# The even layer's out-projection in halves of its rows, the first half beside the neighbourhood attention

## What is computed

```
def _even_mixer(x, norm_g, w_in, ..., rpb_b, w_out):
    h = _rmsnorm(x, norm_g)
    qa, ka, va, qb, kb, vb = _split(h @ w_in, EVEN_SPLITS)
    ...
    oa = _window_gqa(qa, ka, va, sink_a)            # 8 heads of 64: 512 features
    ...
    ob = _neighbourhood_attn(qb, kb, vb, rpb_b)     # 8 heads of 64: 512 features
    return jnp.concatenate([oa, ob], axis=-1) @ w_out   # 1024 x 1024

x = x + _even_mixer(x, ...)
x = x + _mlp(x, mlp_norm[0], w_mlp_in[0], w_mlp_out[0])
```

## Time and profile before

| what | value |
|---|---|
| median of 3 executions | 2370.2 us (2369.26 to 2370.75) |
| the profiled execution, its own time | 2369.17 us |
| its span in the profile | 2367.3 us |
| TensorE busy | 2210.6 us, 93% |
| VectorE busy | 1052.3 us, 44% |
| ScalarE busy | 847.4 us, 36% |
| GpSimd busy | 813.5 us, 34% |
| mean granted TensorE clock | 0.974 |

### The profile page before, as it was taken

The page is one execution under the profiler, slowest core; times in us unless marked ns, Lnnn a source line. Parts: engine busy times, 40 slices in busy tenths (PEclk is TensorE's granted clock), DMA queues, the critical chain, the costliest instruction groups (busy, mean ns, idle before and its releaser), DMA issues.

```text
span 2367.3 us, 27011 instructions
## 1 busy us (share of the span) xinstructions
PE 2210.6 (93%) x9984; PEld 1730.5 (73%) x9984; DVE 1052.3 (44%) x1542; ACT 847.4 (36%) x1256; POOL 813.5 (34%) x343
## 2 busy tenths in 40 slices
PE   6788989779999998898899999999989998999999
PEld 5676357557888885575678888878878876788887
DVE  3456474557552525347533223235562565322221
ACT  5332343443222223345543323343432443433231
POOL 3222013323444442220244444443324322444443
PEclk9899999999999999999999999999999998999999
DMA  4212013112333233110123233232222211223322
GB/s 141 67 54 72 27 45 98 63 45 80 120 111 95 93 129 101 45 63 19 44 91 98 97 95 94 97 105 76 71 67 89 72 63 63 89 98 98 98 98 98
DMA packets 54966, 193.35 MB, mean 82 GB/s; under 512 B 6096, under 2 KB 6352, under 8 KB 54480
## 3 DMA queue, kind: packets, MB, share of 16 engines
q1 hardware_dynamic: 50400, 181.58, 23.5%
q10 hardware_dynamic: 4464, 10.36, 1.3%
HBM read 189.82 MB, written 2.10 MB: 81 GB/s over the span
## 4 chain that ended last, share of the span: by engine, by line
PE 72%; issue 14%; DVE 9%; POOL 4%; ACT 1%; DMA 0%; POOLq 0%; SPq 0%; DVEq 0%; ACTq 0%
PE gemm_ps L493 21%; PE gemm_ps L495 21%; PE gemm_ps L494 21%; POOL wl L462 4%; PE out_ps L860 2%; DVE tmp L1568 1%; DVE arena L1922 1%; DVE tmp L1929 1%; DVE arena L1568 1%; PE turn_ps L688 1%; PE score_ps L679 1%; DVE x L1590 1%; PE out_ps L698 1%; DVE xl L1568 1%; PE score_ps L852 1%
## 5 line engine op out<-in xcount | busy, mean ns | idle before, releaser
L462 POOL TENSOR_TENSOR wl<-raw,wh 128x1024 fp32r<-128x1024 f32 x339 | 813.3, 2401 | 1535.9 <-ACT wh L1086 1535.8
L493 PE MATMUL gemm_ps<-xh,wh 128*128 128x512 f32 x1512 | 615.6, 407 | 55.5 <-DVE xl L1568 22.7
L1086 ACT ACTIVATE wh<-raw 128x1024 fp32r<-128x1024 f32 x339 | 358.7, 1059 | 772.7 <-DMA raw<-w_in 745.3
L494 PE MATMUL gemm_ps<-xl,wh 128*128 128x512 f32 x1512 | 594.5, 393 | 0.0
L495 PE MATMUL gemm_ps<-xh,wl 128*128 128x512 f32 x1512 | 594.3, 393 | 0.0
L494 PE MATMUL gemm_ps<-arena_r,wh 128*128 128x512 f32 (+1 forms) x1124 | 432.1, 384 | 0.0
L493 PEld LDWEIGHTS gemm_ps<-xh,wh 128*128 128x128 f32 x1512 | 288.0, 190 | 137.6 <-issue 56.3
L493 PE MATMUL gemm_ps<-arena_r,wh 128*128 128x512 f32 (+1 forms) x868 | 334.3, 385 | 11.1 <-DVE arena_r L1573 10.2
L494 PEld LDWEIGHTS gemm_ps<-xl,wh 128*128 128x128 f32 x1512 | 287.6, 190 | 66.9 <-issue 9.0
L495 PE MATMUL gemm_ps<-arena_r,wl 128*128 128x512 f32 (+1 forms) x868 | 332.3, 383 | 0.0
L495 PEld LDWEIGHTS gemm_ps<-xh,wl 128*128 128x128 f32 x1512 | 287.2, 190 | 61.5
(11 more groups left out here) (309 smaller groups left out, 2040.2 us busy)
## 6 DMA issues: line engine op xcount, KB each, us to landing
raw<-w_in SPq DMA_DIRECT2D x339, 512.0 KB, 3.3
arena<-na_in ACTq DMA_DIRECT2D x14, 256.0 KB, 2.7
x<-x_in SPq DMA_DIRECT2D x8, 256.0 KB, 6.4
out<-x ACTq DMA_DIRECT2D x8, 256.0 KB, 2.8
arena<-alibi_in ACTq DMA_DIRECT2D x6, 256.0 KB, 3.3
con<-con_in SPq DMA_DIRECT2D x1, 1432.0 KB, 11.7
arena<-moba_in ACTq DMA_DIRECT2D x1, 1024.0 KB, 4.9
arena<-mem_in ACTq DMA_DIRECT2D x1, 1024.0 KB, 4.9
```

The costliest lines, as they stand in the source:

```text
L462: pool.tensor_tensor(wl[:, k, :], raw[:, k, :], wh[:, k, :].bitcast(F32), ALU.subtract).then_inc(unit_split, 1)
L493: pe.matmul(o, wh[:, n % RING, w], h[:, kt, 0:width], start=(kt == 0), stop=False)
L494: pe.matmul(o, wh[:, n % RING, w], l[:, kt, 0:width], start=False, stop=False)
L1086: act.activation(wh[:, k % RING, :], raw[:, k % RING, :], ACT.Copy).then_inc(high_split, 1)
```

## The change

The weights of the even out-projection are put on the stream in another shape: the first four units hold rows 0 to 511 of `w_out`, the last four rows 512 to 1023, and each unit holds two output blocks (2 x 4 input blocks of 128). The first four units run in sixteen pieces of six matmuls in steps 3 to 18 of the neighbourhood attention: two steps for an output block, block `2u` into bank 0 of `gemm_ps`, block `2u + 1` into bank 1. VectorE adds each finished block to `x` in steps 5, 7, ..., 19, behind its own attention work of the step. The last four units follow the attention, two banks each, and their sums are added to `x` a second time. ScalarE raises the units at steps 2, 8, 12, 16 and 19. The meeting of the engines is left out on all three. TensorE waits for the last add of the first half before the second half, and for the last group's split before the last input block of its first unit. The count of matmuls is the same, 192; `x` is added to 16 times in place of 8.

```diff
--- before.py
+++ after.py
@@ -361,6 +361,8 @@
         unit_split = sem("unit_split")
         unit_done = sem("unit_done")
         emptied = sem("emptied")
+        part_done = sem("part_done")
+        part_emptied = sem("part_emptied")
         block_ready = sem("block_ready")
         high_made = sem("high_made")
         proj_raw = sem("proj_raw")
@@ -1007,17 +1009,53 @@
             take(copied_v, 2)
             out = FIRST["even_out"]
 
+            def half_rows(o, n, part, first, start, end):
+
+                for kt in range(start, end):
+                    w = slice((4 * part + kt) * P, (4 * part + kt + 1) * P)
+                    pe.matmul(o, wh[:, n % RING, w], xh[:, first + kt, :], start=(kt == 0), stop=False)
+                    pe.matmul(o, wh[:, n % RING, w], xl[:, first + kt, :], start=False, stop=False)
+                    m = pe.matmul(o, wl[:, n % RING, w], xh[:, first + kt, :], start=False, stop=(kt == 3))
+                return m
+
             def window_part(i):
 
-                if i in (4, 7, 10, 13):
-                    k = (i - 4) // 3
-                    begun(out + k // 2, 2 * (k % 2), 2 * (k % 2) + 2, xh, xl)
+
+                if 3 <= i < 19:
+                    k, later = divmod(i - 3, 2)
+                    u, part = divmod(k, 2)
+                    n = out + u
+                    if later:
+                        half_rows(gemm_ps[:, part, :], n, part, 0, 2, 4).then_inc(unit_done if part else part_done, 1)
+                        return
+                    if not part:
+                        pe.wait_ge(unit_split, n + 1)
+                        if u:
+                            pe.wait_ge(part_emptied, u)
+                        else:
+                            pe.wait_ge(emptied, out)
+                            pe.wait_ge(rhs_ready, blocks_split[0] + 4)
+                    elif u:
+                        pe.wait_ge(emptied, n)
+                    half_rows(gemm_ps[:, part, :], n, part, 0, 0, 2)
             pair_attention(pair_items("neighbour"), window_part)
             blocks_split[0] += 4
-            meet()
-            for n in (out, out + 1):
-                products(n, KT, xh, xl, N, start=4)
-            units(out + 2, KT - 2, xh, xl)
+            groups = taken[group_used]
+            for n in range(out + 4, out + 8):
+                pe.wait_ge(unit_split, n + 1)
+                pe.wait_ge(emptied, out + 4 if n == out + 4 else n - 1)
+                banks = (score_ps[:, n % 2, :], gemm_ps[:, n % 2, :])
+                if n == out + 4:
+                    pe.wait_ge(group_used, groups - 1)
+                    for part, o in enumerate(banks):
+                        half_rows(o, n, part, 4, 0, 3)
+                    pe.wait_ge(group_used, groups)
+                    for part, o in enumerate(banks):
+                        m = half_rows(o, n, part, 4, 3, 4)
+                else:
+                    for part, o in enumerate(banks):
+                        m = half_rows(o, n, part, 4, 0, 4)
+                m.then_inc(unit_done, 1)
             added_sum()
             units(FIRST["mup0"], 1, mh, ml, fresh=True)
             units(FIRST["mup0"] + 1, 7, mh, ml)
@@ -1505,9 +1543,19 @@
                 if 17 <= i <= 18:
                     copy_values([values_b[:, :, k * P:(k + 1) * P] for k in (2 * (i - 17), 2 * (i - 17) + 1)], gemm_ps)
             pair_attention(pair_items("window"), whole=True, between=prepare_neighbour)
-            pair_attention(pair_items("neighbour"))
-            meet()
-            prepare(x, "mlp0", mh, stored(FIRST["even_out"]), added=True)
+            out_first = FIRST["even_out"]
+
+            def raise_out(i):
+                if i == 2:
+                    raise_to(out_first + 3)
+                if i in (8, 12, 16, 19):
+                    raise_to(out_first + 2 + (i + 1) // 4)
+            pair_attention(pair_items("neighbour"), between=raise_out)
+
+            def second_half(b):
+                raise_to(out_first + 4 + b // 2 + 3)
+                act.wait_ge(emptied, out_first + 4 + b // 2 + 1)
+            prepare(x, "mlp0", mh, second_half, added=True)
             mlp("m", 0)
             for p in (1, 2, 3):
                 mlp("m", p)
@@ -2099,9 +2147,25 @@
             def split_window(i):
                 if i < 4:
                     split(y[:, 5 + i, :], xh[:, i, :], xl[:, i, :], rhs_ready)
+                if 5 <= i < 20 and i % 2:
+                    u, part = divmod((i - 5) // 2, 2)
+                    if part:
+                        dve.wait_ge(unit_done, FIRST["even_out"] + u + 1)
+                    else:
+                        take(part_done)
+                    b = 2 * u + part
+                    done(dve.tensor_tensor(x[:, b, :], x[:, b, :], gemm_ps[:, part, :], ALU.add),
+                         emptied if part else part_emptied)
             pair_attention(pair_items("neighbour"), split_window)
-            meet()
-            add(FIRST["even_out"], "mlp0", mh, ml)
+            for u in range(4):
+                n = FIRST["even_out"] + 4 + u
+                dve.wait_ge(unit_done, n + 1)
+                for b, ps in ((2 * u, score_ps), (2 * u + 1, gemm_ps)):
+                    done(dve.tensor_tensor(x[:, b, :], x[:, b, :], ps[:, n % 2, :], ALU.add),
+                         emptied if b % 2 else dve_step)
+                for b in (2 * u, 2 * u + 1):
+                    low(x, "mlp0", mh, ml, b)
+                    add_square(b)
             inverse()
             mlp("m", 0)
             for p in (1, 2, 3):
@@ -2180,7 +2244,10 @@
     e = inp["w_in_e_2"][0]
     units.append(_blocks(np.concatenate([e[:, :512].reshape(D, 8, HD)[:, pair].reshape(D, 512), e[:, 512:]], 1)))
     e = inp["w_out_e_2"][0]
-    units.append(_blocks(np.concatenate([e[:512].reshape(8, HD, D)[pair].reshape(512, D), e[512:]], 0)))
+    a = _blocks(np.concatenate([e[:512].reshape(8, HD, D)[pair].reshape(512, D), e[512:]], 0))
+
+    a = a.reshape(U_EVEN_OUT // 2, 2, P, 2, 4 * P).transpose(3, 0, 2, 1, 4)
+    units.append(a.reshape(U_EVEN_OUT, P, KT * P))
     parts(FF2_PARTS, [inp["w_mlp_in_2"][0]], inp["w_mlp_out_2"][0])
     o = inp["w_in_o_2"][0]
     q, k, v, g = np.split(o, [D, 2 * D, 4 * D], axis=1)
```

## The result

The changed kernel takes 2376.49 us (median of 9 executions, 2374.07 to 2380.71), the kernel before 2369.26 us (median of 9, 2368.05 to 2374.06). The ratio is 1.0030 with a 95% interval of 1.0022 to 1.0038: slower by 0.3%. Forecast were 2369.0 us and no change that can be measured, with 2375 as the upper end. The profiled execution of the changed kernel took 2374.07 us.

The account below looks back on a forecast made before the run. TensorE was taken to bound the out-projection behind the attention, with 8.2 us of holes beside the attention. -16.3 + 12.0 (attention stretch with seam) + 3.6 (tail) = -0.7 us gave 2369.0 us, range 2364 to 2375.

Parts of the forecast that it names:

- the item for the clock at step 3: Attention start: first new piece starts near 1111.8 us, partly at 1.2 GHz, later ones at 2.4 GHz; +0.5 us.
- the item for GpSimd: Attention stretch: GpSimd's low-part subtractions delay VectorE at steps 8, 12 and 16; bounds 0 and 3.8 us, taken 1.3.
- the last: Rival for the whole change: pieces wait for adds or weights; +5 us or more, 2375 and up, chance 0.05.
- the second: Rival: clock falls in the tail before the mlp; with step-16 collision and full backlog 2373.5 to 2377 us, chance 0.2.
- signs of being wrong: Second half starting before 1167.3 or after 1176 us, or the granted clock falling behind the last unit.
- The 72 matmuls: Out-projection behind the attention: 72 matmuls leave the full stretch at 0.227 us each, -16.3 us, called certain.
- A piece costs 1.58 and the floor: Attention stretch: twelve more pieces at 1.58 us add 19.0; with 10.6 us of holes filled, growth is at least 8.4.
- The output steps: Attention steps where VectorE stands 1.61 us for ScalarE: mostly covered by TensorE's longer steps, 0.4 us left in all.
- The adds, the raises' loads, SP: Attention stretch: eight adds on VectorE (5.5 us), and loads for ScalarE's raises on SP, fit in and cost nothing.
- The seam: Between attention and second half: wait for the first half's last add leaves 1.4 us, where 2.4 stood.
- The tail: Last out-projection unit to the mlp: two-block unit delays the column sums by 2.6 us, plus 1.0 backlog; +3.6 us.
- The backlog on VectorE: Tail: VectorE's 4.3 us of work per 5.4 us unit, plus collisions, delays the last adds; bounds 0 and 2.5, taken 1.0.

Follow-up runs that it names:

- e3: Changed kernel with the first piece's waits split and the step-16 raise moved to step 17: ratio to the kernel before 1.0002, stretch 70.9 us.
- e1: Changed kernel, first half of the first piece waits only for the two blocks it reads: ratio to the kernel before 1.0016, stretch 74.3 us.
- e2: Changed kernel with ScalarE's raise of step 16 moved to step 17, so GpSimd's subtraction follows the last division: ratio to the kernel before 1.0016.
- e4: Changed kernel with the first mlp unit's products over six input blocks ahead of the two column sums: ratio to the kernel before 1.0010, tail 23.9 us.

## Why the prediction was wrong

Two terms of the sum for the attention stretch failed: the item for the clock at step 3, which left out the wait for VectorE's fourth split, and the item for GpSimd. The sum for that stretch was +12.0 us and the trace shows +20.2. The measured time lies where two rivals had put it: the last (2375 and up, chance 0.05), with pieces that wait, though for a split and for divisions and not for adds or weights; and the second (2373.5 to 2377, chance 0.2), with the collision at step 16 and the clock's fall in the tail, though smaller and without the backlog. Two of the signs of being wrong came: the second half starts at 1177.19, behind 1176, and the granted clock falls behind the last unit.

- **The 72 matmuls: right.** The stretch behind the attention went from 38.2 to 21.9 us, -16.3.
- **A piece costs 1.58 and the floor: right.** The piece from 1137.90 to 1139.49 takes 1.59. The 0.2 us above six paces lie at its two ends (0.34 us to its second matmul, 0.33 from its last to the scores); that the switch of operand kinds makes them was argued and is not shown. With the two faults mended (e3) the stretch grew by 11.9 us where the sum said 12.0. The waits left there are 3.7 us and the first piece, half of it at 1.2 GHz, takes 0.5 more than 1.58; with the floor of 8.4 that makes 12.6, so the floor holds to within 0.7 us. **The output steps:** 0.4 forecast, and no wait there.
- **The clock item at step 3: wrong, and the largest miss.** I let the first piece start at 1111.8, right behind the values, and gave it 0.5 us. The wait stands in the diff (`rhs_ready`, four blocks), and VectorE's fourth split lies at the end of its step 3. Before, the first piece stood in step 4: it began at 1114.54, the split ended at 1113.79. e1 puts it at 4.9 us: 3.4 of waiting, of which GpSimd's collision at step 3 makes about 1.3, and the rest from the longer spell at half clock. I had counted only the raises at steps 8, 12 and 16 as collisions that matter. I counted the new waits on adds and weights and went past this one.
- **GpSimd beside the attention: 1.3 forecast, 4.8 measured.** I took 1.3 us between 0 and 3.8 and leaned on 80 divisions that were never late. In the trace before only one pair of them meets a subtraction at all: it starts at 286.94, the subtraction 0.40 us behind it, and takes its usual 0.61 us. None had started while a subtraction ran. All three collisions that I named came: 0.7 us at each of steps 9 and 13 (through the negation, not the division), and step 16 at 3.4 us (e2): 1.9 of waiting and 1.5 through the fall of the clock, which I had not put behind it. That is 4.8 in all, above my upper bound; the waiting alone, 3.3, lies within it. The Trainium skill's "SBUF — State Buffer", section "SBUF: two separate sides", has GpSimd and a VectorE operation that uses both of its ports lock each other out for a whole instruction. The trace agrees as far as the time goes: 2.67 in place of 0.74 us; which ports an operation uses no run here shows. The rows that I set against the rule held no case of it.
- **The adds, the raises' loads, SP: right, nothing.** VectorE's eight adds never wait for a piece. **The seam:** 1.4 forecast, 1.66 measured.
- **The tail: right size, other parts.** +3.6 forecast, +4.2 measured (29.6 against 25.4). The first sum came 4.06 us behind the last matmul, as worked out (4.0). The backlog on VectorE (1.0) did not come, VectorE's last two adds start 0.26 us behind the last matmul; the fall of the clock did, the second rival's mechanism. It takes the 1.6 us that remain, 0.9 of them between the two sums (1.87 us apart, in e4 0.96), and not 5, since the clock was back by 1206.5. That the total came near the forecast is luck: one part stood in for the other, and in e1 and e3 the same tail takes 0.7 us more, with the clock down for 6.8 us in place of 3.4.
- **Sum:** -16.3 + 20.2 + 4.2 = +8.1, where -0.7 stood. Of the 8.8 between them 4.9 are the overlooked wait (with the collision at step 3 in it), 3.4 the collision at step 16 (the 1.3 that I took is what steps 9 and 13 cost), 0.6 the tail.

Whether another place of the raises saves the two 0.7 us waits at steps 9 and 13 was not tried, nor was the raise of step 2 moved away from the negation of step 3.

## What to carry to other kernels

When work is moved beside other work, list every wait of the moved piece against the place where its producer stands in the *other* engine's written order; a wait that was free one step later cost 4.9 us here. Rows of an operation that never met the disturbance say nothing of its price: look for the rows in which they overlap, and if there are none keep both ends. And a wait of a few us on TensorE where it bounds is to be priced with the half clock that can follow it; in the tail independent matmuls put into the wait brought 5.7 us (e4), more than the wait of 3.91 itself.

## What the runs showed of the hardware

- A tensor_scalar on 128 x 2 fp32 numbers, 0.17 us alone, took 2.14 and 2.15 us at steps 9 and 13, where it started 0.26 us after a GpSimd subtraction of 128 x 1024, and 1.47 at step 3, where GpSimd was already 0.9 us in. All three ended within 0.03 us of GpSimd's subtraction.
- Reads from PSUM with one SBUF operand (the adds, 0.69 us, and the bias with its maximum, 0.42 us on 256 columns and 0.56 on 384) took no longer beside GpSimd in the changed kernel: six of the adds and eight of the others overlap a subtraction.
- In the changed kernel TensorE's clock fell after a wait of 2.52 us at step 16 (0.50 in 1170 to 1172) but not after 1.66 us at the seam, and in the tail at the end of a wait of 3.91 us. In e1 and e3 it fell 2.1 us into that same wait. Before, a wait of 3.04 us had not made it fall at once. The Trainium skill's "TensorE: Matmul & The Clock Gate", section "What's actually happening", has an idle array at half rate and a busy one released from it; the traces agree in the two levels, 0.50 and 1.00.
